# Returning a spilled residual with transfers that add, and moving five of eight post-norms into the next loop

## The reference

```
f = swiglu(rms_norm(h, ffn_pre_g[i]), w_ff_gate[i], w_ff_up[i], w_ff_down[i])     # D_FF = 2816
h = h + rms_norm(f, ffn_post_g[i])
gate = jax.nn.sigmoid(rms_norm(h, ple_norm_g[i]) @ w_ple_gate[i])
h = h + (p[i] @ w_ple_proj[i]) * gate
```

## Time and profile before

| | |
|---|---|
| median of 3 runs | 2120.76 us (2119.61 to 2121.04) |
| the profiled execution's own time | 2119.99 us |
| its span | 2118.1 us |
| busy: PE, PEld | 2006.9 us (95%), 1646.9 us (78%) |
| busy: DVE, ACT, POOL | 1354.6 us (64%), 748.2 us (35%), 198.3 us (9%) |
| bytes moved | 173.17 MB, mean 82 GB/s |

### The profile page before, as it was taken

The page is one execution under the profiler, slowest core; times in us unless marked ns, Lnnn a source line. Parts: engine busy times, 40 slices in busy tenths (PEclk is TensorE's granted clock), DMA queues, the critical chain, the costliest instruction groups (busy, mean ns, idle before and its releaser), DMA issues.

```text
span 2118.1 us, 27334 instructions
## 1 busy us (share of the span) xinstructions
PE 2006.9 (95%) x9446; PEld 1646.9 (78%) x9446; DVE 1354.6 (64%) x1935; ACT 748.2 (35%) x1369; POOL 198.3 (9%) x232
## 2 busy tenths in 40 slices
PE   6779999999999988999999997999999999999799
PEld 6758888888888867888866685788888888888587
DVE  4886666666666676466579548766666666665942
ACT  3452222333222243243268534333222223332421
POOL 1300000000000043010035311000000000000600
PEclk8889999999999999999999998999999999999999
DMA  4233222233222241121010012333222232334211
GB/s 174 82 99 100 83 83 86 85 99 94 85 84 88 81 178 36 65 105 50 0 41 1 11 60 85 90 100 94 79 89 84 83 90 74 99 99 173 69 42 50
DMA packets 214750, 173.17 MB, mean 82 GB/s; under 512 B 8608, under 2 KB 196384, under 8 KB 214688
## 3 DMA queue, kind: packets, MB, share of 16 engines
q1 hardware_dynamic: 212960, 166.08, 24.7%
q10 hardware_dynamic: 1728, 6.29, 0.8%
HBM read 159.75 MB, written 12.58 MB: 81 GB/s over the span
## 4 chain that ended last, share of the span: by engine, by line
PE 84%; DVE 9%; POOL 3%; issue 2%; ACT 1%; SPq 1%; DMA 0%; ACTq 0%; DVEq 0%; POOLq 0%
PE ps L285 13%; PE ps L287 13%; PE ps L286 13%; PE ps L684 13%; PE ps L686 13%; PE ps L685 13%; PE ps L1364 1%; PE ps L347 1%; PE ps L1306 1%; DVE w_ple_gate_lo L280 1%; POOL probs L1356 1%; DVE t_lo L929 1%; DVE H L1048 1%; DVE small L1315 1%; PE ps L1384 1%
## 5 line engine op out<-in xcount | busy, mean ns | idle before, releaser
L1004 DVE TENSOR_TENSOR H<-H,ps 128x512 f32<-128x512 f32 x320 | 218.1, 685 | 141.8 <-PE ps L287 141.8
L285 PE MATMUL ps<-wd_hi,ffn_a_hi 128*128 128x512 f32 x704 | 275.9, 392 | 9.1 <-DVE H L1004 8.5
L286 PE MATMUL ps<-wd_lo,ffn_a_hi 128*128 128x512 f32 x704 | 274.9, 391 | 0.0
L287 PE MATMUL ps<-wd_hi,ffn_a_lo 128*128 128x512 f32 x704 | 274.9, 390 | 0.0
L684 PE MATMUL ps<-t_hi,s_hi 128*128 128x512 f32 x528 | 207.4, 393 | 20.4 <-DVE t_lo L929 19.0
L685 PE MATMUL ps<-t_lo,s_hi 128*128 128x512 f32 x528 | 206.6, 391 | 0.0
L686 PE MATMUL ps<-t_hi,s_lo 128*128 128x512 f32 x528 | 206.4, 391 | 0.0
L770 ACT ACTIVATE s_hi<-s_raw 128x512 fp32r<-128x512 f32 x176 | 111.3, 633 | 232.7 <-DVE s_raw L893 229.2
L893 DVE TENSOR_TENSOR s_raw<-s_raw,a_raw 128x512 f32<-128x512 f32 x88 | 60.9, 692 | 191.2 <-DMA s_raw<-in_w_ff_gate 145.8
L794 ACT ACTIVATE m<-ps 128x512 f32<-128x512 f32 x44 | 25.9, 589 | 405.0 <-PE ps L686 405.0
L285 PEld LDWEIGHTS ps<-wd_hi,ffn_a_hi 128*128 128x128 f32 x704 | 132.5, 188 | 40.3 <-DVE H L1004 9.2
(11 more groups left out here) (199 smaller groups left out, 4246.3 us busy)
## 6 DMA issues: line engine op xcount, KB each, us to landing
a_raw<-in_w_ff_gate SPq DMA_DIRECT2D x88, 256.0 KB, 2.9
a_raw<-in_w_ff_up SPq DMA_DIRECT2D x88, 256.0 KB, 3.1
s_raw<-in_w_ff_up SPq DMA_DIRECT2D x88, 256.0 KB, 2.9
s_raw<-in_w_ff_gate SPq DMA_DIRECT2D x88, 256.0 KB, 3.2
wd_raw<-in_w_ff_down SPq DMA_DIRECT2D x44, 512.0 KB, 4.1
residual_spill<-H SPq DMA_DIRECT2D x16, 512.0 KB, 2.6
raw<-in_w_ple_gate SPq DMA_DIRECT2D x16, 512.0 KB, 5.4
back<-residual_spill SPq DMA_DIRECT2D x16, 512.0 KB, 5.9
```

The lines of the kernel that those rows point to most:

```text
L285: pe.matmul(out_, lhs[0], rhs[0], start=first, stop=False)
L286: pe.matmul(out_, lhs[0], rhs[1], start=False, stop=False)
L287: return pe.matmul(out_, lhs[1], rhs[0], start=False, stop=last)
L1004: dve.tensor_tensor(dst, dst, ps[:, 4 + n % 4, :], ALU.add).then_inc(F["summed"][n % 4], 1)
```

## The change

1. The eight loads into `back` (SP) and the eight additions (POOL) go, in each layer. In their place POOL issues, behind each scaled tile, a transfer from `residual_spill` that adds itself to the tile of `H` (`accum_op=ADD`). Semaphore `back[j]` now says that tile j has its residual; `post_added` is gone.
2. Tiles 0 to 2 are scaled at the end of the feed-forward; tiles 3 to 7 in the embedding stage's loop, three tiles ahead of the tile that is being multiplied. The loops of that stage are written out on every engine.
3. The row of gains goes to the shared buffer `post_gain`, which overlaps the last buffers of the feed-forward, so its load waits for the last cut of the activations. Two junk buffers and `ple_sig` get other places.
4. The hand-written orders of ScalarE (cuts, squares) and VectorE (`between`) around the end are new. TensorE turns tile 0 behind chunk 12 instead of 14, tile 1 in the middle of the first tile's gate product, and each later tile between the two column halves of the tile ahead.

```diff
         def ffn_post_add(pool, L, j):
 
-            f, n0 = F, TILES * L
-            Hj = H[:, j * D:(j + 1) * D]
-            pool.wait_ge(f["back"][j], 16 * (L + 1))
-            pool.wait_ge(f["scaled"], n0 + j + 1)
-            pool.tensor_tensor(Hj, Hj, Z[f"back{j}"][:, :], ALU.add).then_inc(post_added[L], 1)
+            f = F
+            pool.wait_ge(f["scaled"], TILES * L + j + 1)
+            pool.dma_start(H[:, j * D:(j + 1) * D], spill[L][:, j * D:(j + 1) * D], accum_op=ALU.add
+                           ).then_inc(f["back"][j], 16)
...
             if first_tile:
...
+                    if k == KD // 2 - 1:
+                        turn(pe, s, 0, 1)
...
+                    if c == 0 and 2 * i + p + 1 < TILES:
+                        turn(pe, s, i + (p + 1) // 2, 1 - p)
...
         def ple_act(act, L, i, p):
...
-            if isinstance(i, int) and i == 0 and p == 0:
-                act.wait_ge(post_added[L], 1 + TILES)
...
             def ffn(L):
 
                 fn_rms(pool, L, PAIRS - 1, 1)
-                ffn_post_rms(pool, L, 0)
-                for j in range(1, TILES):
-                    ffn_post_rms(pool, L, j)
-                    ffn_post_add(pool, L, j - 1)
-                    if j in (3, 4):
-                        rms(f"ple{L}")(0, j - 3)
-                ffn_post_add(pool, L, TILES - 1)
+                pool.wait_ge(F["spilled"], 16 * TILES * (L + 1))
+                for j in range(2):
+                    post_tile(L, j)
+                rms(f"ple{L}")(0, 0)
+                rms(f"ple{L}")(0, 1)
+                post_tile(L, 2)
...
-            staggered(pool, [(2, rms("ple0"))], after=[(2, rms("kv"))], head=False)
+            staggered(pool, [(2, rms("ple0")), (3, post(0))], after=[(2, rms("kv"))], head=False, unrolled=True)
...
                 def between(n):
-                    if n in (1, 3):
-                        for k in (n - 1, n):
-                            cut_lo(dve, BASE[f"ple{L}"], k, *[w[:, k, :] for w in w_pg])
-                    if n >= 3 and n % 2:
-                        ffn_post_scale(dve, L, (n - 3) // 2)
-                    if n == 11:
+                    if n == 1:
+                        gate_cut(0)
+                    if n == 3:
+                        ffn_post(dve, L, 0)
+                    if n == 5:
+                        ffn_post(dve, L, 1)
+                    if n == 7:
+                        gate_cut(1)
+                    if n == 9:
                         dve.wait_ge(gain_loaded, 16 * GAIN[f"ple{L}"])
                         normed(dve, s_ple, 0, 0)
+                    if n == 11:
+                        gate_cut(2)
+                    if n == 12:
+                        normed(dve, s_ple, 0, 1)
                     if n == 13:
-                        normed(dve, s_ple, 0, 1)
                         slot_lo(dve, s_ple, 0, 0)
```

More of the change, by code:

```diff
@@ L194, in trunk @@
                    at(100, ("w_ple_gate_lo", [P, KD, D], F32R)),
-                   at(132, *[(f"back{j}", [P, D], F32) for j in range(TILES)]),
                    at(132, *weights("w_kv", [P, KD, 2 * GROUP])),
@@ L527, in trunk @@
         ple_added = [sem_c(f"ple{n}_added") for n in range(2)]
-        post_added = [sem_c(f"ffn{n}_post_added") for n in range(2)]
         def row_load(eng, dst, src, s):
@@ L604, in trunk @@
             "down": sem_c("ffn_down_ready"), "summed": [sem_c(f"ffn_summed{b}") for b in range(4)],
-            "spilled": sem("ffn_spilled"), "back": [sem(f"ffn_back_loaded{j}") for j in range(TILES)],
+            "spilled": sem("ffn_spilled"), "back": [sem(f"ffn_back_added{j}") for j in range(TILES)],
             "ssum2": sem("ffn_out_ssum"), "mean2": sem("ffn_out_mean"), "rstd2": sem("ffn_out_rstd"),
@@ L1504, in ple_loads @@
                 base, last = BASE[f"ple{L}"], (GROUPS - 1, 1)
-                def load_back(j):
-                    sp.dma_start(Z[f"back{j}"][:, :], spill[L][:, j * D:(j + 1) * D]).then_inc(F["back"][j], 16)
                 for k in range(SLOTS):
@@ L1511, in ple_loads @@
                     load_unit(sp, base, k, rows(I["w_ple_gate"][L], k))
-                sp.wait_ge(F["spilled"], 16 * TILES * (L + 1))
-                for name, tiles in (("S2", (2, 3)), ("S1", (0, 1)), ("A22", (4, 5, 6, 7))):
-                    sp.wait_ge(F["product"], nth(name, L, *last))
-                    for j in tiles:
-                        load_back(j)
                 for k in range(SLOTS, KD):
@@ L1596, in _ @@
             ffn(1)
-            staggered(pool, [(2, rms("ple1"))], head=False)
+            staggered(pool, [(2, rms("ple1")), (3, post(1))], head=False, unrolled=True)
         @block.scalar
@@ L1633, in ffn, with gate_cut, tile_squares @@
                 ffn_act(act, L, GROUPS - 1)
-                for k in range(4):
+                def gate_cut(k):
                     cut_hi(act, BASE[f"ple{L}"], k, w_pg[0][:, k, :])
-                for j in range(TILES):
-                    ffn_post_act(act, L, j)
-                    if j in (3, 4):
-                        t = j - 3
-                        act.wait_ge(post_added[L], 1 + t + 1)
-                        square_sum(act, s_ple, 0, t)
-                    if j == 6:
-                        slot_hi(act, s_ple, 0, 0)
-                for k in range(4, KD):
-                    cut_hi(act, BASE[f"ple{L}"], k, w_pg[0][:, k, :])
+                def tile_squares(p):
+                    act.wait_ge(F["back"][p], 16 * (L + 1))
+                    square_sum(act, s_ple, 0, p)
+                gate_cut(0)
+                act.wait_ge(F["a_lo"], 1 + 4 * GROUPS * (L + 1))
+                row_load(act, post_gain, I["ffn_post_g"][L], post_gain_loaded)
+                gate_cut(1)
+                ffn_post_act(act, L, 0)
+                gate_cut(2)
+                ffn_post_act(act, L, 1)
+                gate_cut(3)
+                gate_cut(4)
+                tile_squares(0)
+                gate_cut(5)
+                tile_squares(1)
+                ffn_post_act(act, L, 2)
+                slot_hi(act, s_ple, 0, 0)
+                gate_cut(6)
+                gate_cut(7)
                 act.wait_ge(F["down"], 1 + 16 * GROUPS * (L + 1))
@@ L1656, in ready @@
                 def ready(act, i, p):
-                    act.wait_ge(post_added[L], 1 + TILES)
+                    act.wait_ge(F["back"][2 * i + p], 16 * (L + 1))
                 def cuts(i, p):
@@ L1812, in ple @@
                 staggered(dve, [(1, lambda i, p: slot_lo(dve, s, i, p)), (1, lambda i, p: p_lo(dve, L, i, p)),
-                                (2, lambda i, p: normed(dve, s, i, p)), (0, cuts), (0, lambda i, p: ple_dve(dve, L, i, p))],
-                          after=kv_parts if L == 0 else (), head=False)
+                                (2, lambda i, p: normed(dve, s, i, p)),
+                                (3, of_tile(lambda L, j: ffn_post(dve, L, j), L)), (0, cuts),
+                                (0, lambda i, p: ple_dve(dve, L, i, p))],
+                          after=kv_parts if L == 0 else (), head=False, unrolled=True)
             def q_cut(i, p):
@@ L1902, in _ @@
             ffn(0)
-            ple_parts = [[(1, turned(S[f"ple{L}"])), (0, lambda i, p, L=L: ple_pe(pe, L, i, p))] for L in range(2)]
+            ple_parts = [[(0, lambda i, p, L=L: ple_pe(pe, L, i, p))] for L in range(2)]
             kv_parts = [(1, turned(s_kv)), (0, lambda i, p: kv_pe(pe, i, p)), (-1, lambda i, p: kv_turn(pe, i, p))]
```

55 lines of the change are left out of this document (32 added, 23 removed).

## The result

The changed kernel takes 2084.5 us (median of 4 runs, 2084.3 to 2086.0) where the kernel before took 2120.9 beside it. The ratio, estimated from the single runs and not from the two medians, is 0.9833, 95% interval 0.9821 to 0.9845. The profiled execution has a span of 2082.5 us; before it was 2118.1.

What follows compares the result with a forecast made beforehand. VectorE was taken to bound the two feed-forward ends and TensorE the embedding loop. Each layer gains 21.8 − 6.5 = 15.3 us, 30.6 in all: 2120.0 − 30.6 = 2089.4, predicted as 2089.5, range 2083 to 2107.

Steps and rivals of the forecast that it cites:

- Step 1: End of feed-forward: row of gains, issued behind ScalarE's first cut at 765.2, lands after 5.3 us, at 770.5.
- Step 2: End of feed-forward: tile 0's squares and POOL's factor are done at 768.4, hidden under the gain row by 2.1 us.
- Step 3: End of feed-forward: VectorE's scaling of tile 0, free of POOL, takes 1.28 us, to 771.8.
- Step 4, L: Tile 0's accumulating transfer, from POOL's issue to landing: 6.5 us, from a 5.9 us load plus 0.55 for POOL.
- Step 5: Tile 0's squares, factor and normed row take 3.4 us; TensorE can turn it at 781.7, after waiting 1.9 us.
- Step 6: After tile 0's turn: VectorE's work through the low part takes 6.1 us, TensorE's 5.0, so TensorE waits 1.1.
- Step 7: Eight gate chunks and second turn, 11.0 + 0.85 us, to the projection at 799.7; VectorE's work covered by only 0.9 us.
- The sum: Both ends together: 15.3 us gained in each layer, 30.6 in all, from 2120.0 to 2089.4 us.
- the forecast's own case: Whole kernel: transfer landing in 5 to 9 us gives 2086.5 to 2094.5 us; chance 0.56.
- the rival in which the chain is hidden: Ends: landing up to 4.6 us or early gain row leaves TensorE's floor plus 1.1 us wait, 2083.5 to 2086.5; chance 0.14.
- The signs: Changed profile: 1.28 us scalings, 37 to 38 us ends; wrong if landing exceeds 10 us or tile 0 waits for gain row.
- The loop: Embedding loop: landing plus 4.7 us a tile hides under TensorE's 14.6; from 10.2 us landing, each microsecond costs six per layer.

Runs made afterwards that it cites:

- the run with the low part first: Changed kernel with VectorE making tile 0's low part ahead of tile 1's normed row, and tile 0 turned behind chunk 13 instead of 12: 2083.2 us.
- the two delaying runs: Changed kernel with one, or two, unused awaited transfers ahead of those of tiles 3 to 7; with two, 0.7 to 1.0% slower than the kernel before.
- the order alone: Changed kernel's orders and moved scalings, but SP's residual loads and POOL's additions as in the kernel before: ratio to that kernel 0.9834 to 0.9865.

## Why the prediction was right, step by step

All times are counted from the first down product of layer 0, which stood at 761.90 when I predicted and stands at 760.70 now.

- **Step 1, the row of gains.** Predicted there at 8.6 us; it landed in 3.7 us instead of 5.3, and tile 0 was scaled from 7.0. The chain was 1.6 us ahead of the prediction by it. I took 5.3 from the kernel before, where such rows travel beside other loads; with those gone it was quicker in every run without loads of the residual (3.4 to 3.8), and 4.3 us in the one that kept them.
- **Step 2, the squares.** Right: they were hidden under the row of gains, but by 0.4 us and no longer by 2.1. POOL had tile 0's factor at 767.4, and VectorE waited for the row until 767.7.
- **Step 3.** Right: 1.28 us, on every scaling of every run but the kernel before (1276 to 1289 ns).
- **Step 4, L.** From the end of the scaling (769.02) to the squares (775.09) it took 6.1 us, 0.33 of it until POOL issued; I had 6.5. By the view of transfers it is 5.5. The estimate of 3.2 us worked out from the Trainium skill (DMA: Bandwidth & Descriptors, Anatomy of one DMA) was too low even for the plain transfer, 3.9. The other rule weighed, that VectorE holds POOL's issuing, did not show: an issue took 884 to 1025 ns, in the end and in the loop alike. The Trainium skill (SBUF — State Buffer, SBUF: two separate sides) states that rule for VectorE operations in a two-port mode, a condition that the prediction left out; whether any operation here runs in such a mode, no run shows.
- **Step 5.** 3.4 us, as predicted. Tile 0's row was ready at 17.83 where I had 19.8; 1.6 + 0.4 explain it. TensorE gets there by itself at 17.80, and the turn started at 17.89. The wait of 1.9 us shrank to a tie, with nothing to spare. That it came out so even is luck: the prediction had no reason for it.
- **Step 6.** The gate product waits 0.66 us in layer 0 and 0.83 in layer 1, predicted 1.1. It stands 5.86 us behind the turn, predicted 6.1. In kind this was right, and the run with the low part first took it away.
- **Step 7.** From the first gate product to the projection 11.91 us, predicted 11.9. VectorE's cover was about as thin as said: the small operation that the projection needs ended at 795.06, 1.3 us ahead of it (predicted 0.9), and in the low-part-first run it came 0.3 late.
- **The sum.** An end of 37.8 us was predicted and 35.66 and 35.78 measured, 2.1 and 2.0 less. With the 1.2 us gained ahead of the first end, which the prediction did not foresee, this makes the 5.0 us or so. The time is inside the range, but the forecast's own case (chance 0.56) did not come true. The term that was too large is step 1, the landing of the row of gains: what came true is the rival in which the chain is hidden (2083.5 to 2086.5, chance 0.14), with L at 5.5 to 6.1 and not under 4.6, and with the fast row of gains, which that rival named as the other way to it. By an estimate from the same steps, a row that landed in 5.3 us would have made each end 1.6 us longer, and the time would have been inside the forecast's own range.
- **The signs.** The prediction gave as a sign of being wrong that the row of gains takes POOL's place as what tile 0 waits for. That is what the profile shows: tile 0's scaling is released by the row, 0.33 us late, in both layers. Steps 1 and 2 had foreseen this, so the sign was badly chosen. The ends of 37 to 38 us and the wait of some 2 us on the turn did not show; the other signs did.
- **The loop.** In kind confirmed by the two delaying runs: hidden in the changed kernel and, but for 1.7 us in one layer, at 9.8; 26.5 and 24.9 us a layer, 20.5 and 19.5 of them waits, at a mean of 15.7 and 15.4. In size the formula was too kind: its chain of 4.7 us beside the transfer is 5.4, which over five tiles is 3.5 us of cover less.
- **What was incomplete.** I gave VectorE's hold and the eight scalings as two reasons and took the change as one thing. The halves replace each other: the order alone is worth 15.2 and 16.3 us of 17.4 and 17.2. I also followed tile 0 only. Tile 1's squares stand on ScalarE ahead of tile 0's cut, and with slower transfers it is they that the gate waits for.

## What to carry to other kernels

Where two engines slow each other, count what it is worth to part them in time before replacing the operation: here the new order with its moved scalings had nine tenths of the gain without any new kind of transfer. When a load is turned into a transfer behind a computation, write its latency L into each chain that has it and compute the L at which each cover ends; the chain that repeats (six times a layer here) decides whether the change may turn into a loss. And follow the second item of each in-order queue too, not only the one that the bound waits for.

## What the runs showed of the hardware

- Adding to the target costs a transfer of 512 KB 1.6 us of landing: 5.5 against 3.9 us, both issued by POOL. POOL is occupied for 0.9 to 1.0 us by issuing the first kind, 0.6 to 0.7 for the plain one.
- Transfers of 512 KB that overlap slow each other: 5.5 us in the median, 8.3 and 8.7 for one issued behind two others that were under way (7.8 in the other layer). With six in one stretch POOL stood still for 3.9 and 3.75 us at the sixth. That this is a limit of its queue was not tested further.
- The same waits of TensorE (0.89, 0.66 and 2.3 us) were followed by some 3.5 us at the clock's lower level in one layer and by 1.00 in the other, in one execution. What decides it stays open; it was worth 1.6 us.
- A POOL addition of 2.4 us took 8.2 us once while VectorE cut weights beside it, and a cut beside another addition 2.43 instead of 1.22. In the end of the kernel before it was the scalings that paid, 3.04 for 1.28.
